# The gate stage of both layers: six plain tiles and five seven-product pairs instead of sixteen plain tiles

## What is computed

```python
for i in range(DEPTH):                      # DEPTH = 2
    hn = _rmsnorm(h, norm_g[i])
    u = hn @ w_in[i]
    ...                                     # convolution branch ya, windowed attention yb
    h = h + jnp.concatenate([ya, yb], axis=-1) @ w_out[i]
    e = _rmsnorm(p[i] @ w_pe[i], pe_g[i])
    h = h + e * jax.nn.sigmoid(h @ w_pg[i]) # w_pg[i] is 2048 x 2048: the gate stage
```

## Time and profile before

| | us |
|---|---|
| median of 3 runs | 2524.79 (2524.76 to 2526.66) |
| the profiled execution's own time | 2524.99 |
| its span, first to last instruction | 2523.2 |
| PE busy in it | 2515.8 (100%) |
| DVE, ACT, POOL busy | 1549.4 (61%), 1066.7 (42%), 1324.5 (52%) |
| gate stage of layer 0 on PE | 711.27 to 885.80 |

### The profile page before, as it was taken

The page is one execution under the profiler, slowest core; times in us unless marked ns, Lnnn a source line. Parts: engine busy times, 40 slices in busy tenths (PEclk is TensorE's granted clock), DMA queues, the critical chain, the costliest instruction groups (busy, mean ns, idle before and its releaser), DMA issues.

```text
span 2523.2 us, 40982 instructions
## 1 busy us (share of the span) xinstructions
PE 2515.8 (100%) x15264; PEld 2130.5 (84%) x15264; DVE 1549.4 (61%) x2510; ACT 1066.7 (42%) x1618; POOL 1324.5 (52%) x1668
## 2 busy tenths in 40 slices
PE   9999999999999999999999999999999999999999
PEld 7888888889988888888878899888888888899887
DVE  7977766575462387777665745634654655955722
ACT  6212365643462342223655434634322656545421
POOL 6555554443355555555454434555666776534554
PEclk9999999999999999999999999999999999999999
DMA  7322243248733333223432487233322323388322
GB/s 251 114 92 99 97 123 113 91 144 210 165 108 125 116 118 101 98 94 101 120 114 95 162 188 171 92 133 114 112 98 94 101 92 100 98 188 241 101 95 105
DMA packets 95424, 313.56 MB, mean 124 GB/s; under 512 B 9456, under 2 KB 25584, under 8 KB 92208
## 3 DMA queue, kind: packets, MB, share of 16 engines
q1 hardware_dynamic: 75264, 268.45, 31.6%
q0 software_dynamic: 10368, 37.75, 8.6%
q10 hardware_dynamic: 9648, 5.36, 1.0%
HBM read 297.86 MB, written 16.81 MB: 125 GB/s over the span
## 4 chain that ended last, share of the span: by engine, by line
PE 99%; DMA 0%; ACT 0%; DVE 0%; issue 0%; SPq 0%; POOL 0%; DVEq 0%; ACTq 0%
PE acc L2070 18%; PE acc L2071 18%; PE acc L2072 17%; PE sc L2071 6%; PE sc L2070 6%; PE sc L2072 6%; PE sc L2340 2%; PE sc L2341 2%; PE sc L2342 2%; PE acc L2340 1%; PE acc L2341 1%; PE acc L2342 1%; PE acc L2094 1%; PE sc L2094 1%; PE sc L2096 1%; PE sc L2100 1%
## 5 line engine op out<-in xcount | busy, mean ns | idle before, releaser
L792 POOL TENSOR_TENSOR WL<-raw,WH 128x256 fp32r<-128x256 f32 x1504 | 1195.0, 827 | 907.6 <-ACT WH L852 907.3
L2070 PE MATMUL acc<-XH,WH 128*128 128x512 f32 x1936 | 756.4, 391 | 0.1
L2071 PE MATMUL acc<-XL,WH 128*128 128x512 f32 x1936 | 753.7, 389 | 0.0
L2072 PE MATMUL acc<-XH,WL 128*128 128x512 f32 x1936 | 753.3, 389 | 0.0
L852 ACT ACTIVATE WH<-raw 128x1024 fp32r<-128x1024 f32 x378 | 398.9, 1058 | 795.2 <-PE acc L2072 538.6
L2070 PEld LDWEIGHTS acc<-XH,WH 128*128 128x128 f32 x1936 | 363.4, 188 | 80.5 <-issue 4.9
L2072 PEld LDWEIGHTS acc<-XH,WL 128*128 128x128 f32 x1936 | 363.5, 188 | 76.0
L2071 PEld LDWEIGHTS acc<-XL,WH 128*128 128x128 f32 x1936 | 363.5, 188 | 74.3
L2070 PE MATMUL sc<-XH,WH 128*128 128x512 f32 x640 | 249.0, 389 | 0.0
L2071 PE MATMUL sc<-XL,WH 128*128 128x512 f32 x640 | 249.0, 389 | 0.0
L2072 PE MATMUL sc<-XH,WL 128*128 128x512 f32 x640 | 249.0, 389 | 0.0
(11 more groups left out here) (425 smaller groups left out, 4408.3 us busy)
## 6 DMA issues: line engine op xcount, KB each, us to landing
raw<-in_w SPq DMA_DIRECT2D x416, 512.0 KB, 3.3
raw<-in_w POOLq DMA_DIRECT2D x54, 512.0 KB, 6.2
a<-in_w POOLq DMA_DIRECT2D x18, 512.0 KB, 5.9
a<-in_w SPq DMA_DIRECT2D x16, 512.0 KB, 7.6
h_spill<-H SPq DMA_DIRECT2D x8, 1024.0 KB, 6.1
H<-h_spill SPq DMA_DIRECT2D x8, 1024.0 KB, 8.2
a<-bias_band SPq DMA_DIRECT2D x16, 384.0 KB, 3.7
H<-in_x SPq DMA_DIRECT2D x5, 1024.0 KB, 7.6
```

Of the source, the lines that this page charges most:

```text
L792: part = pool.tensor_tensor(WL[:, c], raw[:, c], WH[:, c].bitcast(F), ALU.subtract)
L2070: pe.matmul(bank, WH[:, c], xh, start=first, stop=False)
L2071: pe.matmul(bank, WH[:, c], xl, start=False, stop=False)
L2072: return pe.matmul(bank, WL[:, c], xh, start=False, stop=last)
```

## The change

The gate stage of each layer becomes six plain tiles and five pairs (35 products, `P_STEPS`).

- The tiles' order is 0 to 3, 14, 15, then the pairs' tiles in the order in which they are complete (`g_tile`).
- The sums of `H` halves for the pairs are made by DVE and ACT during the plain tiles: `sum_adds`, `third_add`, `sum_lows`, `third_low` and the `fourth` parts.
- They take the place of `e` in `Y`. So `e` is stored to HBM (`e_store`, four transfers of 1 MB) and comes back one tile at a time (`e_load`, 256 KB) into two small buffers, `acc` and `rs`, and for the last two tiles into `Y`.
- A fifth weight buffer, `wa2`, is taken from the fourth slot of `WL`. Low parts of the pairs go round three slots. DVE makes the low part of step j+2 in its iteration j (it was j+3 in the output stage); POOL makes those of `p2` and `p7` (nine of the 35).
- `gate` reads the plain products straight from PSUM with a scale of 0.5: `halve` is gone.
- `H` is stored tile by tile (`h_store`, 256 KB) instead of in four transfers, and SP issues these between the pairs' loads.

The diff, cut to its core:

```diff
-A_U, KV_U, Z_U, OUT_U, PE_U, PG_U = 48, 8, 32, 8, 4, 32
+A_U, KV_U, Z_U, OUT_U, PE_U, PG_U = 48, 8, 32, 8, 4, 12
+P_PLAIN = 6
+P_PAIRS = 5
+P_STEPS = (
+    ("p2", 0), ("p1", 0), ("p5", 0), ("p3", 0), ("p1", 1), ("p6", 0), ...
+def p_low_slot(j):
+    return RING - 1 if j == P_N - 1 else (j + 2) % (RING - 1)
+        WA2 = nc.alloc_sbuf_tensor_at("WA2", [P, UW], F, offset=nc.lookup_mloc(WL).addr + (RING - 1) * UW * 4)
...
+                first_load(("p1", 2))                       # SP
+                first_load(("p2", 1))
+                sp.wait_ge(sum_tail, 16 * ly + parts_begun(4))
+                e_load(1)
+                first_load(("p2", 0))
+                e_load(2)
+                first_load(("p1", 0))
+                e_load(3)
+                e_load(4)
+                for n in range(3):
+                    h_store(n)
+                e_load(5)
+                h_store(3)
...
+                    if j in P_SIDE:                         # POOL
+                        pool.wait_ge(fast_high, fast_base(ly) + j + 1)
+                        pool.wait_ge(*p_wl_free(ly, j))
...
+                    if p_next(j) is not None and not p_loads(p_next(j)):
+                        pool.wait_ge(*p_low_made(ly, j))
+                        pool.dma_start(P_PLACE[name], w[p_unit(ly, *P_STEPS[p_next(j)])], accum_op=ALU.add)...
...
+                square(0)                                   # ACT
+                square(1)
+                prep(u0, PG0 + 6)
+                prep(u0, PG0 + 7)
...
+                block_prep(2)
+                square(4)
+                gate(5)
...
+                gated(4)                                    # DVE
+                block_lows(1)
+                for c in range(4):
+                    dve.wait_ge(sum_head, s0 + 10 + c + 1)
+                    dve.tensor_tensor(sums_of(4, True)[:, 2 * c:2 * c + 2, :], fourth(c),
+                                      sums_of(4, False)[:, 2 * c:2 * c + 2, :].bitcast(F), ALU.subtract).then_inc(sum_tail, 1)
+                block_lows(0)
+                sums(4)
...
-                quad_tile(n0 + N_PG, u0 + PG0, 0, x0 + 2 * NT)   # PE
-                ...
-                quads(n0 + N_PG, u0 + PG0, 1)
+                for t in range(P_PLAIN):
+                    if t >= 2:
+                        pe.wait_ge(g_th, ly * NT + t - 1)
+                    unit(...)
+                for j, (kind, q) in enumerate(P_STEPS):
+                    pe.wait_ge(*p_low_made(ly, j))
+                    ...
```

More of the change, by code:

```diff
@@ new lines, in p_close, with p_first, p_loads, p_count @@
+def p_close(j):
+    return any(p_place(*P_STEPS[i]) == p_place(*P_STEPS[j]) for i in range(max(0, j - 3), j))
+def p_first(j):
+    return all(p_place(*P_STEPS[i]) != p_place(*P_STEPS[j]) for i in range(j))
+def p_loads(j):
+    return P_STEPS[j][0] in ("p1", "p2", "p3")
+def p_count(name, loads, n=P_N):
+    return sum(p_place(*P_STEPS[i]) == name and p_loads(i) == loads for i in range(n))
+def p_rows_before(j, part):
+    kind, q = P_STEPS[j]
+    return max((i for i in range(j) if P_STEPS[i][1] == q and part in rows_of(P_STEPS[i][0])), default=None)
@@ L187, with g_done, place_before @@
+def g_done(n):
+    return p_done(*P_ORDER[n - P_PLAIN])
+def place_before(n):
+    return max(i for i in range(n) if g_place(i) == g_place(n))
+SPLITS = range(P_PLAIN, NT)
+TAIL_N = NT - 2
 BLOCKS = (1, 2, 0, 3)
@@ new lines, in _ @@
+                square(0)
+                square(1)
+                prep(u0, PG0 + 6)
+                prep(u0, PG0 + 7)
+                gate(3)
+                square(2)
+                block_prep(0)
+                square(3)
+                block_prep(1)
+                gate(4)
+                act.wait_ge(w_used, u0 + PG0 + P_U - 1)
+                act.wait_ge(sum_whole, s0 + 14)
+                for c in range(4):
+                    act.activation(sums_of(4, False)[:, 2 * c:2 * c + 2, :], fourth(c), ACT.Copy).then_inc(sum_head, 1)
@@ L1153, in xc_high @@
+                for t in range(UT, NT):
+                    if t == UT + 2:
+                        square(NT - 1)
+                    xhigh(t, tl(H, t), norm_col(ly + 1, t))
             def xc_high(g):
@@ L1766, in _ @@
+                block_outs(P_N - 1)
+                sums(NT - 3)
+                scaled(NT - 1)
+                next_low(4)
+                next_low(5)
+                gated(NT - 1)
+                sums(NT - 2)
+                for k in range(6, 10):
+                    next_low(k)
+                sums(NT - 1)
+                for k in range(10, NT):
+                    next_low(k)
             xb = DEPTH * 3 * NT
```

586 lines of the change are left out of this document (445 added, 141 removed), and 4 rows, old and new, of the table P_STEPS.

## The result

The changed kernel takes 2541.39 us (median of 4 runs, 2538.20 to 2544.41), the kernel before, on the same chip, 2524.78. The ratio is 1.0063, with a 95% interval of 1.005 to 1.0077: slower by 16.6 us. I had forecast 2525, with 2512 to 2538 as the range.

What follows compares the result with a forecast made beforehand. PE was taken as the bound, everything else hidden. From 2524.99 us: minus 16.0 saved, plus 5.6 (layer 0 stalls), 9.4 (layer 1) and 1.0 (inside the pairs) gave 2525.0, range 2512 to 2538.

Steps and rivals of the forecast that it cites:

- What PE saves: Gate stage, each layer: 480 matmuls of 512 columns replaced by 840 of 256, saving 8.0 us a layer, 16.0 in all.
- The start of the pairs: PE waits before products 0, 2, 5 and 6 for late low parts: 5.6 us in layer 0, 8.9 in layer 1.
- Inside the pairs: Stalls when buffers are used again after three products: 1.0 us for both layers, bounded by 0 and 18.
- The end of the stage: Layer 1's end: DVE, about 3 us behind with sums, gives the next stage its low parts late; about 0.5 us.
- Rival C: PE's clock falls after stalls at the pairs: up to 3.5 us for each of two, time 2532; chance 0.04.
- Rival B: DMA engines become the bound in the pairs, share 0.98 or 0.94: time about 2540, from 2531 up; chance 0.22.
- the play of 3 us: Slack in the pairs from DVE being up to two products ahead; gone when a landing takes 8 us instead of 6.2.

Runs made afterwards that it cites:

- e7: Changed kernel with e1's and e2's edits, two small reorderings, e6's DVE moves, and all low parts on DVE; 2514.35 us, ratio 0.9958.
- e1: Changed kernel with SP's loads of e tiles 1 to 4 ahead of the weight loads they stood behind, both layers; 2529.15 us, ratio 1.0014.
- e5: Changed kernel with DVE making all 35 low parts of the gate's pairs, including the nine POOL made; 2530.50 us.
- e6: Changed kernel with e1's and e2's edits, two small reorderings, and three moves more in the orders of DVE and POOL; 2526.57 us.
- e13: e7 with 5 subtractions on POOL's own buffer at each place where POOL had made a low part; 2518.45 us.
- e14: e7 with only the low parts of products 32 and 33 back on POOL, both layers; 2520.10 us.
- e2: Changed kernel with ACT's next-stage high parts moved ahead of other work, and DVE's six next-stage low parts two products earlier; 2537.64 us.
- e4: Changed kernel with 16 of 20 tile moves a layer out of the pairs, leaving out part of the computation (timing alone); 2532.57 us.
- e11: e7 with 12 subtractions on POOL's own buffer at each place where POOL had made a low part; 2566.19 us.

## Why the prediction was wrong, step by step

**What PE saves: right.** 16.0 us. The spacing in the gate's pairs is 0.1200, and e7, with 3.6 us of stalls and low clock left, ran 11.3 us under the kernel before in its profiled execution, where 16.0 - 3.6 would be 12.4.

**The start of the pairs: right in its mechanism, and in its sum partly by luck.** I had 14.5 us in both layers; it was 14.9. Product by product in layer 0: 1.4, 1.8, 1.5, 0.9 foreseen, 2.6, 1.8, 1.3, 1.0 measured; e tile 2 foreseen at 764.1, landed at 765.2. In layer 1 it was 3.0, 2.6, 2.4, 0.9 foreseen and 4.4, 1.2, 1.6, 1.0 measured, 8.9 against 8.2. A chain walked in written order, with durations of rows, held within 1.4 us at each product, and the errors had both signs: layer 0 came out 1.1 over, layer 1 0.7 under. e1 shows the cause of product 0's stall.

**Inside the pairs: mis-sized, 1.0 against 6.0.** The step that failed is the sentence that the steps whose low part is POOL's leave DVE none to make in that iteration. I counted POOL's low parts as relief for DVE. They are on PE's path themselves (2.8 to 3.1 us for 1.22), they stand ahead of accumulations in POOL's list, and one DVE operation in each layer met them after all (4.19 and 4.16). e5 took them away, and the middle went to 0.0; in all POOL's low parts cost 10.9 us in the changed kernel, and 12.2 between e6 and e7. Of that, e13 puts some 4 on POOL's time being taken, and e14 puts some 6 on the low parts of products 32 and 33. These two overlap, and their shares are known only to 2 us or so; how the rest divides between late low parts and a slowed DVE stays open, since in e13 neither was there.

**The end of the stage: the worst miss, 0.5 against 6.4.** I looked at the low parts of `XL` on DVE. What came last was the next stage's second weight unit. ACT's timeline, then POOL's:

```profile
882.48 1.04 ACT L1128 ACTIVATE WH<-raw 128x1024 fp32r<-128x1024 f32 x1
883.43 1.32 ACT L1148 ACTIVATE XH<-H,v 128x512 fp32r<-128x512 f32 x2
884.65 0.61 ACT L1406 ACTIVATE T<-T 128x512 f32<-128x512 f32 x1
885.18 1.04 ACT L1128 ACTIVATE WH<-raw 128x1024 fp32r<-128x1024 f32 x1
```

```profile
883.60 9.47 POOL L1052 TENSOR_TENSOR WL<-raw,WH 128x256 fp32r<-128x256 f32 x11 [3.62 <-ACT WH L1128]
```

Product 31 freed the first unit's slot at 879.1 and product 32 the second's at 882.0; ACT made their high parts at 882.48 and 885.18, behind other work of its list, and the second low part was done at 890.5, against 887.8 when PE was free. Between the freeing of that slot and the next stage lie two products of 2.88 now, where two units of 5.44 lay before: half the time for the same work. My walk stopped at the last product instead of going on to the next stage's first. That the order of the lists made this wait is shown by e2, which took it to 0.5 and 0.1; e4 points to late landings as a part of it.

**The low clock: left out of the sum, 7.4.** Rival C had it as a case of its own with a chance of 0.04 and a price of 7. It is not a case beside the others but what a stall costs besides. (Its sentence that no wait of the kernel before is longer than 0.65 us passed over the 1.50 at the kernel's start, in the same.) Layer 1, after product 0's wait:

```profile
1666.32 0.58 PE L2841 MATMUL sc<-XH,WH 128*128 128x256 f32 x1 [4.23 <-DVE WL L2110]
1666.70 0.41 PE L2842 MATMUL sc<-XL,WH 128*128 128x256 f32 x1
1666.91 0.41 PE L2843 MATMUL sc<-XH,WL 128*128 128x256 f32 x1
```

After 4.23 us of waiting, 14 matmuls of 256 columns came 0.213 apart instead of 0.120; after 3.34 us, 12 of 512 columns 0.427 apart; after 2.73 us, 7; after 2.45 us, before product 0 of layer 0, one. The Trainium skill (TensorE: Matmul & The Clock Gate, section What's actually happening) has the array go from 2.4 to 1.2 GHz once it has been idle, and the trace agrees in both levels.

The length of the wait alone doesn't tell whether the clock falls. In e11 PE waited 3.31 us before product 26 of layer 1 and the clock stayed up; in e2 it waited 1.78 before product 2 of layer 0, after 2.46 before product 0, and 17 matmuls came 0.213 apart. Start of the product and window, e11 and then e2 (PE's clock is the third number from the end):

```profile
1734.96 0.39 PE L2856 MATMUL sc<-S,WH 128*128 128x256 f32 x1 [3.31 <-DVE WL L2125]
1734.00:1740.00 6.00, 5.04 (x42) 5.04 (x43) 5.97 (x10) 4.34 (x7) 2.76 (x6) 1.00 0.57 102
```

```profile
786.72 0.39 PE L2844 MATMUL acc<-S1H,WH 128*128 128x256 f32 x1 [1.78 <-DVE WL L2115]
786.00:790.00 4.00, 3.29 (x20) 3.29 (x21) 4.00 (x6) 1.10 (x2) 1.73 (x2) 0.75 0.77 183
```

So the 7.4 is a measured sum of this execution, and the runs give no rule by which it could have been forecast.

**Rival B had the time (2540) and not the mechanism.** The share rose only to 0.87, accumulations landed in 6.9 to 7.0 us on the mean and 9.2 at most, and e7 ran at 0.95 in layer 0's pairs without a stall. (Its own terms gave 18 us in the pairs, and my sum took 16.) But my note for it, that long landings eat the play of 3 us, was sound: either POOL's low parts or the tile moves could be taken away, and the middle fell to 0.0 (e5) or 1.4 (e4). It took both to make most of it. That the forecast of 2525 was so wrong while its largest term was right is the sum of three omissions of one sign.

## What to carry to other kernels

Making the bound engine's steps shorter shortens every deadline around them: walk the new chain past the stage's last step, into the first work of the next stage, since that reuses the slots freed last. A helper engine that takes work off another may lengthen the path it is on; count its duration as latency, and everything behind it in its list. An order list that waits in the middle holds what is ready behind it, and moving that load was the cheapest edit here (12 us). Give the clock behind stalls a term of its own with a range: here it was 0 to 3 us for a stall of 2 to 4 us.

## What the runs showed of the hardware that I had not expected

PE's clock fell after waits of 2.73, 3.34 and 4.23 us in the middle of the changed kernel and cost 1.5 to 3 us more each, but not after one of 3.31 in e11. DVE and POOL hold each other up, and either can be the one that is held. A DVE low part begun beside POOL's, 128x256 each, took 4.19 us where one alone takes 1.22; POOL's operation on 128x88 took up to 1.4 us beside a DVE low part where one alone takes 0.33, and that low part kept its 1.22 (e11). The Trainium skill (GPSIMD Engine Reference, section Specifications) has the two share their interface to SBUF where a DVE operation has two inputs there, and the trace agrees. The kernels with stalls were less steady in their times: in one and the same comparison the 25 runs of the kernel before spread over 5 us and the ten of e6 over 10.
